# A sorted list of expert items entered by direct jumps, with TensorE's far branches announced ahead

## What is computed

```python
def _swiglu(x, wg, wu, wd):
    h = jax.nn.silu(jnp.einsum('bld,df->blf', x, wg)) * jnp.einsum('bld,df->blf', x, wu)
    return jnp.einsum('blf,fd->bld', h, wd)
...
    flat_e = top_i.reshape(-1)
    order = jnp.argsort(flat_e)
    tok = order // TOP_K
    xs = xt[tok]
    sizes = jnp.bincount(flat_e, length=N_EXPERTS).astype(jnp.int32)
    h = jax.nn.silu(lax.ragged_dot(xs, wg, sizes)) * lax.ragged_dot(xs, wu, sizes)
    ys = lax.ragged_dot(h, wd, sizes) * top_w.reshape(-1)[order][:, None].astype(x.dtype)
    y = jnp.zeros_like(xt).at[tok].add(ys)
```

## Time and profile before

| | us |
|---|---|
| runs (3) | 5300.23 median, 5287.87 to 5302.04 |
| the profiled execution | 5294.93 |
| its span, first to last instruction | 5293.3 |
| PE busy | 5000.5 |
| DVE busy | 3409.7 |
| ACT busy | 1600.8 |
| mean granted PE clock | 0.968 |

### The profile page before, as it was taken

One profiled execution on the slowest core, in us unless ns is written; L12 is line 12 of the kernel. 1 busy time (PEld: TensorE's weight loads), 2 busy tenths in 40 slices (PEclk: granted clock), 3 DMA queues, 4 the chain that ended last, 5 costly groups with the idle time before them and its releaser, 6 DMA issues. The chain is left out here.

```text
span 5293.3 us, 86729 instructions
## 1 busy us (share of the span) xinstructions
PE 5000.5 (94%) x33128; PEld 4921.8 (93%) x33129; DVE 3409.7 (64%) x5297; ACT 1600.8 (30%) x2280; POOL 404.5 (8%) x246
## 2 busy tenths in 40 slices
PE   8999999999998999999959999999999899989969
PEld 7999999999998999999959999999989898989958
DVE  5677756444456656965557676566668686866665
ACT  2112222111113311122224443333335444433333
POOL 3111101111002211110010000000000000000020
PEclk8999999999999999999979999999999999999979
DMA  2111111111111111111045444444446555544431
GB/s 94 49 45 40 41 38 41 48 47 43 48 41 44 47 47 38 48 40 42 16 174 177 163 166 155 146 143 149 151 139 202 170 186 169 196 160 148 143 121 41
DMA packets 399007, 528.53 MB, mean 100 GB/s; under 512 B 12056, under 2 KB 353606, under 8 KB 398616
## 3 DMA queue, kind: packets, MB, share of 16 engines
q1 hardware_dynamic: 359552, 460.75, 26.1%
q0 software_dynamic: 11136, 33.97, 1.9%
q10 hardware_dynamic: 27928, 28.60, 1.6%
HBM read 494.87 MB, written 28.39 MB: 99 GB/s over the span
## 5 line engine op out<-in xcount | busy, mean ns | idle before, releaser
L1478 DVE TENSOR_TENSOR WLO<-WRAW,WHI 128x1024 fp32r<-128x1024 f32 x866 | 1065.8, 1232 | 286.5 <-ACT WHI L1110 178.8
L659 PE MATMUL PS<-XHI,WHI 128*128 128x384 f32 (+1 forms) x3648 | 1202.2, 330 | 4.1 <-DVE ACC L1987 2.5
L661 PE MATMUL PS<-XHI,WLO 128*128 128x384 f32 (+1 forms) x3648 | 1197.2, 328 | 0.0
L660 PE MATMUL PS<-XLO,WHI 128*128 128x384 f32 (+1 forms) x3648 | 1196.6, 328 | 0.0
L1110 ACT ACTIVATE WHI<-WRAW 128x1024 fp32r<-128x1024 f32 x866 | 898.9, 1051 | 945.3 <-PE PS L765 681.0
L659 PE MATMUL PS<-XSH,WHI 128*128 128x232 f32 (+7 forms) x3584 | 1066.1, 297 | 52.4 <-issue 39.7
L661 PE MATMUL PS<-XSH,WLO 128*128 128x232 f32 (+7 forms) x3584 | 1062.9, 297 | 0.0
L660 PE MATMUL PS<-XSL,WHI 128*128 128x232 f32 (+7 forms) x3584 | 1061.3, 296 | 0.4 <-issue 0.3
L659 PEld LDWEIGHTS PS<-XSH,WHI 128*128 128x128 f32 x3584 | 685.8, 191 | 57.0 <-issue 52.4
L659 PEld LDWEIGHTS PS<-XHI,WHI 128*128 128x128 f32 x3648 | 690.9, 189 | 7.3 <-DVE ACC L1987 3.3
L660 PEld LDWEIGHTS PS<-XLO,WHI 128*128 128x128 f32 x3648 | 690.7, 189 | 0.7
(11 more groups left out here) (367 smaller groups left out, 5781.5 us busy)
## 6 DMA issues: line engine op xcount, KB each, us to landing
WRAW<-in_moe_w_gate SPq DMA_DIRECT2D x112, 1024.0 KB, 4.9
WRAW<-in_moe_w_up SPq DMA_DIRECT2D x112, 1024.0 KB, 4.9
WRAW<-in_moe_w_down SPq DMA_DIRECT2D x112, 1024.0 KB, 4.7
WRAW<-in_w_in SPq DMA_DIRECT2D x48, 1024.0 KB, 5.2
WRAW<-in_ffn_w_gate SPq DMA_DIRECT2D x11, 1024.0 KB, 5.2
WRAW<-in_ffn_w_up SPq DMA_DIRECT2D x11, 1024.0 KB, 5.2
WRAW<-in_ffn_w_down SPq DMA_DIRECT2D x11, 1024.0 KB, 4.8
XG<-sorted_rows POOLq DMA_DIRECT2D x18, 512.0 KB, 4.7
```

The source lines that it names most:

```text
L659: pe.matmul(PS[:, bank, 0:n], wh, hi(k), start=(k == 0), stop=False)
L660: pe.matmul(PS[:, bank, 0:n], wh, lo(k), start=False, stop=False)
L661: ins = pe.matmul(PS[:, bank, 0:n], wl, hi(k), start=False, stop=(k == KC - 1))
L1478: v.do(dve.tensor_tensor(WLO[s][:], raw_view(conv.n // 2 % RAW, conv.n % 2, kind), WHI[s][:].bitcast(F32), ALU.subtract), conv)
```

## The change

- PE's tree is replaced. All eight experts' own items run in a loop written with labels: at its head (`item_begin`) the size is loaded, a chain of compares finds the class and marks there, for the announcement of a branch, the location (`mark_branch_hint_location`, used by `.branch_hint`) ahead of the first unit; then comes the first gate/up unit at 336 rows; then a second chain of compares jumps straight into the body of that size. A body does all else at its own size but the last down product, which is behind the bodies, at 336 rows. The jump out of a body is announced ahead of its last four gate/up units, the jump back to the head ahead of the last down product.
- Extra items have a loop of their own, ahead, of 6 passes with a condition around the body, all at 336 rows. The register holds the number of extra items (`extras`), on all engines.
- On ACT and DVE likewise: a loop of 6 passes with a condition for extra items, then a loop of 8 without one. The three parts of `item_out` move from the four units of group 0 to those of group 1, on PE, ACT and DVE. SP and POOL keep one loop of 14 passes.
- `MOE_LOOP` is 5 in place of 6: two more groups are written out.
- The loop of the dense channel mixer on PE announces its back edge at its head (`hint_back_edge=True`).

The diff on PE; ACT and DVE are changed in the same way, their steps moved out of the loop and called from both loops:

```diff
-    FFN_LOOP, MOE_LOOP = (FFN_GROUPS - 3) // 2, (MOE_GROUPS - 2) // 2
+    FFN_LOOP, MOE_LOOP = (FFN_GROUPS - 3) // 2, (MOE_GROUPS - 4) // 2
...
-                with pe.Fori(0, FFN_LOOP) as i:
+                with nc.Fori(0, FFN_LOOP, engines=[pe.engine], hint_back_edge=True) as i:
...
-                n_items = pe.value_load(ITEMS[0:1, L_NUM:L_NUM + 1], min_val=NE, max_val=SLOTS)
+                extras = pe.value_load(ITEMS[0:1, L_NUM:L_NUM + 1], min_val=0, max_val=SLOTS - NE)
...
+                last = MOE_GROUPS - 1
+                def gate_up(rows):
+                    use()
+                    b = open_bank()
+                    product(b, rows, unit.n % HL, lambda k: XSH[:, k, 0:rows], lambda k: XSL[:, k, 0:rows]).then_inc(q.next(), 1)
+                    unit.n += 1
+                def add_down(rows, g, after=lambda d: None):
+                    pe.wait_ge(S["split_done"], hs.take(2))
+                    down(EHI[g % 2], ELO[g % 2], ((0, rows),), after)
+                def item(rows, begun=0, after=lambda d: None):
+                    for u in range(begun, 4):
+                        gate_up(rows)
+                    for u in range(4):
+                        gate_up(rows)
+                        if u < len(XBLK):
+                            item_out(u)
+                    with pe.Fori(0, MOE_LOOP) as i:
+                        cs2 = [unit, q, hs]
+                        per2 = {unit: 12, q: 24, hs: 4}
+                        st2 = looped(cs2, i, per2)
+                        for g in range(2):
+                            add_down(rows, g)
+                            for u in range(4):
+                                gate_up(rows)
+                    leave(cs2, st2, per2, MOE_LOOP)
+                    add_down(rows, last - 3)
+                    for u in range(4):
+                        gate_up(rows)
+                    add_down(rows, last - 2)
+                    leaving = pe.mark_branch_hint_location() if begun else None
+                    for u in range(4):
+                        gate_up(rows)
+                    add_down(rows, last - 1, after)
+                    return leaving
+                with pe.Fori(0, SLOTS - NE) as it:
+                    with pe.If(it < extras):
+                        st = looped(cs, it, per)
+                        q_item = q.at(q.n)
+                        pe.wait_ge(S["xg_ready"], it * 48 + 48)
+                        for k in range(KC):
+                            prepare(k)
+                        pe.wait_ge(S["split_done"], hs.take(KC))
+                        item(CAP)
+                        add_down(CAP, last)
+                        leave_items(cs, st, per, extras)
+                pe.wait_ge(S["xg_ready"], extras * 48 + 48)
+                spacer(pe)
                 for k in range(KC):
                     prepare(k)
-                with pe.Fori(0, SLOTS) as it:
-                    with pe.If(it < n_items):
-                        size = pe.value_load(ITEMS[0:1, bass.ds(it + L_SIZE, 1)], min_val=0, max_val=len(SIZES) - 1)
-                        st = looped(cs, it, per)
...
-                        def begin(rows, depth):
-                            gate_up(rows, depth)
-                            if depth < len(XBLK):
-                                item_out(depth)
-                        def end(rows, depth):
-                            if depth == 3:
-                                gate_up(rows, 2)
-                                gate_up(rows, 3)
-                            elif depth == 2:
-                                pe.wait_ge(S["xg_ready"], it * 48 + 96)
-                                add_down(rows, last - 1, range(0, 4), prepare)
-                            elif depth == 1:
-                                add_down(rows, last - 1, range(4, KC), prepare)
-                            else:
-                                add_down(rows, last, range(0, 4))
...
-                        def choose(low, high, depth):
-                            if depth < 4:
-                                begin(SIZES[high - 1], depth)
-                            if high - low == 1:
-                                item(SIZES[low], depth)
-                                return
-                            middle = (low + high) // 2
-                            here = [c.n for c in cs]
-                            with pe.If(size < middle):
-                                choose(low, middle, depth + 1)
-                                end(SIZES[middle - 1], depth)
-                            for c, n0 in zip(cs, here):
-                                c.n = n0
-                            with pe.If(size > middle - 1):
-                                choose(middle, high, depth + 1)
-                                end(SIZES[high - 1], depth)
-                        pe.wait_ge(S["split_done"], hs.take(KC))
-                        choose(0, len(SIZES), 0)
-                        add_down(CAP, last, range(4, KC))
-                        leave_items(cs, st, per, n_items)
+                turn = nc.alloc_registers("pe_expert", engines=[pe.engine])
+                nc.regs_mov(turn, 0)
+                pe.br("item_begin")
+                with nc.body("item_begin", valid_engines=[pe.engine]):
+                    e = nc.snap(turn, min_val=0, max_val=NE - 1)
+                    place = extras + e
+                    size = pe.value_load(ITEMS[0:1, bass.ds(place + L_SIZE, 1)], min_val=0, max_val=len(SIZES) - 1)
+                    st = looped(cs, e, per)
+                    q_item = q.at(q.n)
+                    def choose(low, high, do, stage):
+                        if high - low == 1:
+                            do(SIZES[low])
+                            return
+                        middle = (low + high) // 2
+                        names = [f"{stage}_{low}_{middle}", f"{stage}_{middle}_{high}"]
+                        pe.br_lt(size, middle, on_true=names[0], on_false=names[1])
+                        for name, x, y in zip(names, (low, middle), (middle, high)):
+                            with nc.body(name, valid_engines=[pe.engine]):
+                                choose(x, y, do, stage)
+                    ahead = {}
+                    def announce(rows):
+                        ahead[rows] = pe.mark_branch_hint_location()
+                        pe.br("item_announced")
+                    choose(0, len(SIZES), announce, "announce")
+                    nc.switch_bb("item_announced")
+                    pe.wait_ge(S["split_done"], hs.take(KC))
+                    gate_up(CAP)
+                    here = [c.n for c in cs]
+                    choose(0, len(SIZES), lambda rows: pe.br(f"item_{rows}").branch_hint(ahead[rows]), "enter")
+                    for rows in SIZES:
+                        for c, n0 in zip(cs, here):
+                            c.n = n0
+                        with nc.body(f"item_{rows}", valid_engines=[pe.engine]):
+                            def fetch_next(d):
+                                if d == 0:
+                                    pe.wait_ge(S["xg_ready"], place * 48 + 96)
+                                prepare(d)
+                            left = item(rows, 1, fetch_next)
+                            pe.br("item_end").branch_hint(left)
+                    nc.switch_bb("item_end")
+                    again = pe.mark_branch_hint_location()
+                    add_down(CAP, last)
+                    nc.regs_alu(turn, turn, 1, op=ALU.add)
+                    pe.br_lt(turn, NE, on_true="item_begin", on_false="items_end").branch_hint(again)
+                nc.switch_bb("items_end")
+                leave(cs, st, per, NE)
...
+                with act.Fori(0, SLOTS - NE) as it:
+                    with act.If(it < extras):
+                        row = act.value_load(ITEMS[0:1, bass.ds(it + L_ROW, 1)], min_val=0, max_val=PAIRS)
+                        st = looped(cs, it, per)
+                        kp[0] = LOOK
+                        for k in range(KC):
+                            prepare(k)
+                        step(*first, convert)
+                        step(*second, convert)
+                        item_out(it, row)
+                        m.n += 6
+                        for s in (*middle, late, last):
+                            step(*s, convert)
...
+                with act.Fori(0, NE) as e:
+                    place = extras + e
+                    row = act.value_load(ITEMS[0:1, bass.ds(place + L_ROW, 1)], min_val=0, max_val=PAIRS)
+                    st = looped(cs, e, per)
+                    kp[0] = LOOK
+
+                    def conv():
+                        ahead = kp[0] - 2 * len(item_kinds)
+                        if ahead >= 0:
+
+                            with act.If(e > NE - 2):
+                                act.wait_ge(S["folded"], fold.at(fold.n + 1 + ahead // 2))
```

(32 more changed lines are left out.)

191 lines of the change are left out of this document (68 added, 123 removed).

## The result

The changed kernel takes **5229.76 us** in the median of 4 runs (5221.69 to 5237.87), the kernel before 5300.78 in the median of its 4 runs beside them (5287.87 to 5302.04): a ratio of 0.9871 with a 95% interval of 0.9849 to 0.9894, so 71 us or 1.3% faster. The forecast was 5152 with a range of 5126 to 5232: the sign was right, the size a little under half of what was expected (71 us for 148), and the time stands at the very edge of the range. The profiled execution took 5225.91 us for a span of 5224.3.

The account below looks back on a forecast made before the run. PE was taken as the bound, with only its instruction waits and slow clock to win. Items 2156.8 + 8 + 15 + 4.6 = 2184.4 against 2321.6, then -5, +1, -2: -143 from 5294.93 gives 5152 us, range 5126 to 5232.

Parts of the forecast that it names:

- The undisturbed 2156.8 us: Ideal PE time of the eight items under the new schedule, built from uninterrupted groups, against 2321.6 us before.
- Step 1: Three announced far jumps an item replace PE's tree: 1 us left an item, 8 us in all, ends 0 and 26.
- step 3: DVE, with ACT ahead of it, late at item boundaries: 15 us over the eight items, ends 7 and 60.
- Step 2: Size loaded and compared twice on PE's instruction stream behind 48 queued matmuls: costed at nothing.
- Step 4: First item starts cold: lower clock and one wait for T cost about 4.6 us, and stay.
- Step 5: Six false passes move ahead of the first item: 5 us won behind the last item, 1 lost ahead of the first.
- Step 6: Dense loop's three back edges, announced a whole body ahead: 2 us won, ends 0 and 2.5.
- The announcement does nothing, or comes too late: Rival, chance 0.17: three plain far jumps an item remain, 11 us an item instead of 1, total 5232 us.
- Its dearest end: That rival's costliest variant: jumps with slow clock cost 17 us an item, 136 in all, total 5280 us.
- a DVE or ACT bound: Rival, chance 0.08: DVE and ACT bound the item boundary, 60 us in place of 15, total 5197 us.
- a false-pass miss: Rival, chance 0.04: 12 far jumps ahead of the first item miss at 4.4 us each, total 5197 us.
- The slower case: Rival, chance 0.05: announced blocks push out inner-loop code, 40 back edges cost up to 6.9 us each, total 5428 us.

Follow-up runs that it names:

- e6: e3 with the eight transposes of the next item's rows spread, four over the next-to-last down product and four over the last: 5170.09 us.
- e10: e6 with its two announcements an item taken out: 5233.97 us, ratio 0.9877 to the kernel before.
- e1: The changed kernel without its three announcements an item, dense loop still announced: 5283.78 us, ratio 0.9969 to the kernel before.
- e5: e3 with the next item's size loaded inside the body, behind the inner loop, into a register of its own: 5190.02 us.
- e12: e1 with the eight transposes spread over the last two down products, timed in rounds: 5216.02 us, ratio 0.9834 to the kernel before.
- e2: The changed kernel with only the dense loop's back edge unannounced: 5234.68 us in a single run.
- e3: The changed kernel with its item loop turned: next size loaded and body announced ahead of the last down product, no jump back: 5192.49 us.
- e4: The changed kernel with the item loop's head and the code behind the bodies each moved to an address boundary: 5219.45 us, one run.
- e11: The changed kernel with the exit announced 48 matmuls and eight transposes ahead of the jump in place of 144 matmuls: 5231.25 us.

## Why the prediction was right or wrong

- **The bound** was right, and where the time lies: PE's instruction stream was what could be won, DVE and ACT did not become the bound, and most of the gain is in the items (60.2 of 69.0). The undisturbed 2156.8 us were some 9 to 17 us too low (the busy time at the full clock that every version has over them), and otherwise held up: e6 comes within 2202.9 - 2156.8 = 46 of it, of which 25 are idle and 8 lower clock.
- **Step 1, the residue of the jumps, is the step that failed.** It had 8 us, with ends 0 and 26. Measured are 25.7 (jump back, seven items) + 6.2 (jump in) + 11.2 (jump out), 43 us of idle time, and most of the 19.5 us that the lower clock costs from the second item on: up to 62.5 us against 8. That is some 54 of the miss of 77 in the items (2261.4 - 2184.4). Of the rest 17 us are the ideal's, which was too low, and 5 step 3's. Three things were wrong in it. The price was taken from the dense loop's back edge (1.1 us at most), while e10 and e1 price an unannounced far jump of this loop at 3 to 10 us. A gap was charged without the slow clock behind it, although the boundary's own rows showed that a gap of 4.5 us costs 7. And "cover plus what is queued is about enough" was said of all three alike; only the jump out was helped much (57.5 to 11.2 us), and three exits stayed at 2.0 to 3.6 us. The jump in, with 24 matmuls of lead, gained nothing from its announcement (9.0 against 7.4 us without), the jump back with 48 gained 4.
- **Step 2, size load and compares at nothing:** too low by some 0.7 us an item for the load where it is exposed (e5); the compares weren't measured by themselves.
- **Step 3, DVE and ACT late:** 15 us forecast, 16.0 ahead of the transposes + 3.6 in the bodies = 19.6 measured. Right within its bounds. But its indirect price was missed: those waits, 0.3 to 1.9 us each, stand just ahead of the jump out, and without an announcement the jump costs 57.5 us with them and 14.9 without (e1, e12). That they do it by emptying PE's queue fits this and isn't shown by itself.
- **Step 4, first item:** 4.6 forecast, 4.7 measured: 2.87 us of wait ahead of its second unit, and 1.8 that the lower clock costs up to 2733.4 us.
- **Step 5, false passes:** the tail gained 8.3 us for 5 forecast. What had stood at 6.54 is now
```profile
4992.03 1.06 PE L960 MATMUL PS<-IDF,EACC 128*128 128x128 f32 x8 [0.89 <-DVE EACC L2246]
```
  The head lost 2.8 us for 1 forecast. It is ACT that comes late, out of six false passes, 3.7 us behind the transposes that it waits for (they start at 2715.16), where before it was waiting for them:
```profile
2718.86 1.28 ACT L1357 ACT_TABLE_LOAD   x1 [9.34 <-issue]
```
- **Step 6, the dense loop:** 2 us forecast, 3.2 measured to the landmark. The three waits of 2.5 us in all are gone, and e2 brings them back (2.1).
- **The rivals.** "The announcement does nothing, or comes too late" was the right one, at 0.17. It put the gaps with their slow clock at 11 us an item and the time at 5232; measured are up to 62.5 / 8 = 7.8 and 5229.8. That its time fits to 2 us is in part luck, since the ideal that it was added to was 17 us too low. That an announcement does little is true of two of the three; that it comes too late is the likely reason and isn't shown for the jump back. Its dearest end, no help at all, stood at 5280, and e1 takes 5283.8. Only the places were taken wrongly: it had the item's start dear and the exit cheap, and without announcements the exit is the dear one (57.5 us against 39.0 for both gaps at the start), where the list gathers all eight transposes, with their waits for the split, right ahead of it. The rule of the Trainium skill (Runtime: NRT & Kernel Launch, Instruction fetch mechanics), that a taken branch out of the current two-page window forces a fetch before execution goes on, agrees with the unannounced jumps of e10, which cost 3.0 to 5.6 us with matmuls queued. An announced jump with 72 matmuls of lead doesn't pay it (0.0 us in e3 and e6). A window of two pages isn't what PE's dense loop shows once its back edge is announced: a pass of 144 us for which the kernel before reads some 9 blocks (28 in 455 us) runs without a read, so here the measurement decides.
  The rivals of a DVE or ACT bound and of a false-pass miss did not come. The slower case, in which an announced block pushes code out that is still needed, is not seen (its break-even would have been 22 of the 40 edges, 148 / 6.9, not 21): the bodies have no gap at their inner back edges, and the items read fewer blocks, not more (86 against 101 from 2735 to 4935 us).
- **The range.** Its lower end of 5126 is not what its own terms give: residues of 0 and 7 make 5152 - 8 - 8 = 5136. It changes nothing here, since the time came out at the other end.

## What to carry to other kernels

A far jump of PE's instruction stream was seen here at three prices: none, where it is announced 72 matmuls (11 us at 336 columns) ahead; 1.1 to 5.6 us, unannounced with matmuls ahead of it that don't wait; 6.5 to 10.3 us, unannounced right behind semaphore waits. With less lead than 72 matmuls, or with stalls in between, an announcement helped some jumps and not others. To each us of gap came 0.2 to 0.5 us that the lower clock cost (21.3 for 66.0 in the changed kernel). So before announcing a jump, move waits away from it, and turn the loop so that the decision about the next pass is made ahead of the last long piece of work of this one: that was worth 60 us on top of the change here (e6: 5170.1 us, 2.4% below the kernel before). And price what is left of such a change from the gaps of the same loop, with their slow stretches, not from the cheapest jump elsewhere in the trace.

## What was not expected of the hardware

- Announcing a back edge lowers the number of instruction blocks that are read at all, 43 to 16 in 760 us of the dense loop, and 28 to 0 between 1030 and 1485 us, while the passes do the same work; it is not only a matter of when they are read.
- A jump announced 144 matmuls ahead can still cost 2.0 to 3.6 us, and which one does changes when two places of the code are aligned (e4); 48 matmuls ahead, the same three are exposed, at 3.2 to 4.0 us (e11). In each exposed one a block of instructions is read only then, from 2.9 to 3.4 us before the work behind the jump starts.
- An unannounced jump right behind waits for a semaphore costs up to 10.31 us, where the longest issue wait at PE's products in the kernel before was 5.6.
